# Seven weight slots, each at an address offset of its own, in a float32 transformer kernel on one core

## The chip, the cores and the metric

The kernel runs on one NeuronCore of a Trainium2 chip. The metric is the device time of one execution in microseconds, from the first instruction to the last with what lies around them. The engines are TensorE (PE in the profile; its weight loads are the row PEld), VectorE (DVE), ScalarE (ACT), GpSimd (POOL) and SyncE (SP), which here only issues loads. SBUF is the on-chip memory of 128 partitions in which all operands of this case lie.

## What is computed

Three transformer blocks follow each other on 256 tokens of width 2048, all in float32. The first is attention (two kinds of heads, with 256 tokens of context beside), the second a Fourier mixer, the third a mixer of a gated delta rule and dilated attention, with a convolutional gated MLP behind it. Cut to the lines that hold nearly all of the arithmetic, the reference is a row of products of activations with weight matrices:

```python
def attn_project(h, ...):            # first block, for x and for ctx
    z = h @ w_in                     # 2048 x 4928
def gated_out(y_a, y_b, gate, w_out):
    return (y * jax.nn.silu(gate)) @ w_out
def fourier_mixer(h, w_in, w_out):   # second block
    u, gate = jnp.split(h @ w_in, 2, axis=-1)          # 2048 x 8192
    f = jnp.fft.fft2(ug, axes=(1, 3), norm="ortho").real
    return (f * jax.nn.silu(gate)) @ w_out             # 4096 x 2048
def token_mixer(n, ...):             # third block
    proj = jnp.einsum("bsd,dp->bsp", n, w_in)          # 2048 x 13344
    ...
    return jnp.einsum("bsm,md->bsd", mixed, w_out)
def conv_gated_mlp(n, w_ffn_in, conv_ffn_w, w_ffn_out):
    up = depthwise_conv_centered(jnp.einsum("bsd,df->bsf", n, w_ffn_in), conv_ffn_w)  # 2048 x 11264
    gate, val = jnp.split(up, 2, axis=-1)
    return jnp.einsum("bsf,fd->bsd", jax.nn.silu(gate) * val, w_ffn_out)              # 5632 x 2048
```

## The kernel before, in words

**Units.** All weights of these products are packed on the host into 478 units of at most 1 MB: 128 partitions by up to 2048 float32, which is four slices of 128 input rows by 512 output columns, or two or three slices of 768 columns. `UNITS` (line 206) is the list in the order in which they are used, and each of the engines' programs walks through it in this order.

**Slots.** SBUF is one slab of 53,100 float32 per partition. Its first 7 × 2048 words are the weight slots, laid out by `W.place(UNIT)` (lines 466 to 468): four raw ones, into which units are loaded, and three high ones. Behind them are a region `K` of 9360 words that is kept through the kernel, and a region `R` that each block lays out anew; activations are there, each buffer at a multiple of 8 words from the region's start (`place`, line 449). Unit number u uses raw slot u modulo 4 and high slot u modulo 3 (`RAW_OF`, `HIGH_OF`, lines 264 and 265). In the head (the first 44 units) there are six raw slots and four high ones: two more raw slots and one more high slot lie in `R`, the high one at word 40080 of the slab, the raw ones at words 42128 and 51048 (lines 504 to 511); there the slots go by u modulo 6 and u modulo 4.

**A unit's way.** SyncE waits until the raw slot's previous unit is used and loads the next one (line 621). ScalarE casts it to float32r, a shortened float32, into the high slot (`act_hi`, line 1155). VectorE subtracts the high part from the raw one and writes the rest, also float32r, over the raw slot (`dve_lo`, line 1665). Both run two or three units ahead of TensorE. The activations are split in the same way into a high and a low half, for most of the kernel in `Hhi` and `Hlo` (words 27792 and 23696 of the slab). TensorE (`pe_unit`, lines 648 to 652) then does three matmuls for each slice and each 128 output columns:

```python
hi = unit_cut(high[HIGH_OF[u]][1], u)[:, kt - k0, :]
lo = unit_cut(raw[RAW_OF[u]][1], u)[:, kt - k0, :]
mm(e, o, *operands(kt, i, hi, 0), first, False)
mm(e, o, *operands(kt, i, hi, 1), False, False)
ins = mm(e, o, *operands(kt, i, lo, 0), False, last)
```

For most products the 128 × 128 piece of weights is the stationary operand (loaded by a LDWEIGHTS of its own) and the activations are the moving one, of 256 columns. For the products `fu`, `dv` and a few others it is the other way round. Each matmul instruction of the trace has one weight load in front of it, which TensorE does while the matmul before it runs.

**Order.** Nothing is planned at run time: each engine's program is written out, with semaphores between. Smaller work (norms, attention, the Fourier products, the delta rule) stands between units of the long products or in gaps of its own. The last stretch, `ff` and `oX` from 2601 us on, is 6,336 matmuls of 256 columns with nothing between them.

Of the kernel before, what the change touches and what calls it, by code (L numbers as in the profile page):

```python
# [9 lines left out]
F32 = mybir.dt.float32  # L10
F32R = mybir.dt.float32r
# [8 lines left out]
UNIT = 2048  # L20
SLOTS = 4
HIGH = 3
A_SCALE = (128 + 64) ** -0.5
B_SCALE = 128 ** -0.5
SLAB = 53100
KEEP = 9360
ALPHA = 4.0 ** 0.25
EPS = 1e-6
# [367 lines left out]
def program(nc, a, out, cmaps):  # L396
    with ExitStack() as ctx:
# [7 lines left out]
        base = -(-nc.sbuf_base // 32) * 32  # L405
        ctx.enter_context(nc.sbuf_tensor("slab", [128, SLAB], F32))
        pieces = {}

        def piece(o, n, dt):
            if (o, n, dt) not in pieces:  # L410
                name = f"{'r' if dt == F32R else 'f'}_{o}_{n}"
                pieces[(o, n, dt)] = nc.alloc_sbuf_tensor_at(name, [128, n], dt, offset=base + 4 * o)
            return pieces[(o, n, dt)]
# [49 lines left out]
                named["all"] = v  # L463
                return named

        W = Region(0, UNIT * (SLOTS + HIGH))
        raw = [W.place(UNIT) for _ in range(SLOTS)]
        high = [W.place(UNIT) for _ in range(HIGH)]
        K = Region(W.size, KEEP)
        R = Region(W.size + KEEP, SLAB - KEEP - W.size)  # L470

# [1893 lines left out]
```

## Time and profile before

| | us |
|---|---|
| median of the timed runs (three) | 3376.86 |
| lowest and highest of them | 3375.43, 3382.23 |
| profiled execution, its own time | 3346.91 |
| its span, first to last instruction | 3345.1 |
| TensorE busy in it | 3122.8 |
| VectorE busy | 1871.0 |
| ScalarE busy | 1266.4 |

The profiled execution is one more execution of the same program; what lies around its span is 1.8 us. Busy time is the union of an engine's instructions. Matmuls overlap in the trace, since the next one begins before the one before has drained: a stretch in which TensorE is busy throughout can still be denser or less dense. How dense it is, is told by the count of matmuls in a window of known width. A count in a window includes the instructions that reach over its edges, two or three more than begin in it.

### The profile page before, as it was taken

The numbers are of one execution on the slowest core, as the hardware profiler recorded it, in microseconds if no ns is written. First come the engines' busy times: TensorE is split into PE (matmuls) and PEld (weight loads), VectorE is DVE, ScalarE is ACT, GpSimd is POOL, SyncE is SP. The second block draws the span as 40 slices with busy tenths as digits, with TensorE's granted clock in tenths as the row PEclk, the third lists the DMA queues.
The fourth block names the chain that finished last, engine by engine and source line by source line (L and its number), as shares of the span: only waits on it lengthen the run. The fifth ranks groups of instructions, "written<-read, shape, count | busy, mean of one in ns | idle before, by whom it ended". The sixth has DMA issues, their size and how long they took to land.

```text
span 3345.1 us, 52152 instructions
## 1 busy us (share of the span) xinstructions
PE 3122.8 (93%) x23130; PEld 2854.4 (85%) x23130; DVE 1871.0 (56%) x2119; ACT 1266.4 (38%) x1310; POOL 211.2 (6%) x180
## 2 busy tenths in 40 slices
PE   6999879987899999979999999999979899999998
PEld 3699765586888998969999989978869899999998
DVE  6736664465765434455545444764544666557753
ACT  7623231133333333343433333432223444334433
POOL 0000000000000000001112110013400000000000
PEclk9999899998999999999999998999989999999999
DMA  8745544343465454424444434520004455555553
GB/s 333 290 168 216 189 167 155 126 175 149 189 247 193 173 183 161 150 100 161 162 155 151 159 125 152 186 92 1 1 28 174 156 197 187 195 199 191 199 188 130
DMA packets 81632, 548.01 MB, mean 164 GB/s; under 512 B 9568, under 2 KB 9600, under 8 KB 28160
## 3 DMA queue, kind: packets, MB, share of 16 engines
q1 hardware_dynamic: 69984, 466.91, 39.3%
q0 software_dynamic: 9216, 67.11, 5.4%
q10 hardware_dynamic: 2208, 10.65, 0.8%
q8 instruction: 183, 3.00, 0.4%
q14 instruction: 41, 0.34, 0.0%
HBM read 542.54 MB, written 2.10 MB: 163 GB/s over the span
## 4 chain that ended last, share of the span: by engine, by line
PE 86%; DVE 6%; issue 3%; DMA 3%; ACT 2%; SPq 0%; DVEq 0%; ACTq 0%
PE bank L631 84%; DMA f<-in_later 2%; DVE f L1694 1%; DVE r L1665 1%; ACT r L1155 1%; PE bank L679 1%; DMA f<-in_units 1%; PE bank L920 0%; DVE f L1882 0%; DVE f L1713 0%; DVE f L2091 0%; ACT f L1267 0%; DVE f L1980 0%; DVE f L1904 0%; DVE f L1836 0%
## 5 line engine op out<-in xcount | busy, mean ns | idle before, releaser
L631 PE MATMUL bank<-r,r 128*128 128x256 f32 (+4 forms) x19360 | 2427.8, 287 | 88.0 <-issue 41.5
L631 PEld LDWEIGHTS bank<-r,r 128*128 128x128 f32 (+3 forms) x19360 | 2320.9, 188 | 192.4 <-issue 103.8
L1665 DVE TENSOR_TENSOR r<-f,r 128x2048 fp32r<-128x2048 f32 (+2 forms) x466 | 1012.6, 2175 | 915.8 <-ACT r L1155 914.4
L1155 ACT CAST r<-f 128x2048 fp32r<-128x2048 f32 (+2 forms) x466 | 835.7, 1795 | 1057.5 <-PE bank L631 856.4
L631 PE MATMUL bank<-f,f 128*128 128x128 f32 (+10 forms) x3258 | 660.5, 356 | 82.7 <-ACT f L1334 14.8
L631 PEld LDWEIGHTS bank<-f,f 128*128 128x128 f32 (+5 forms) x3258 | 474.2, 195 | 211.4 <-issue 112.3
L1694 DVE SCALAR_TENSOR_TENSOR f<-f,f,f 128x512 f32<-128x512 f32 x240 | 180.2, 751 | 52.1 <-DMA f<-in_later 45.3
L1167 ACT COPY f<-bank 128x512 f32<-128x512 f32 (+2 forms) x141 | 80.3, 588 | 152.4 <-PE bank L631 146.7
L2029 DVE SCALAR_TENSOR_TENSOR f<-f,f,f 128x255 f32<-128x255 f32 (+1 forms) x272 | 131.6, 484 | 9.7
L679 PEld LDWEIGHTS bank<-f,f 128*128 128x128 f32 x288 | 39.3, 166 | 69.1 <-issue 24.2
L2280 POOL DMA_DIRECT2D f<-in_later x64 | 34.0, 531 | 1013.9 <-DVE f L1694 844.4
L679 PE MATMUL bank<-f,f 128*128 128x128 f32 x288 | 51.5, 321 | 39.8 <-ACT f L1316 13.8
L2289 POOL TENSOR_TENSOR f<-f,f 32x512 f32<-32x512 f32 x24 | 30.9, 1286 | 821.2 <-PE bank L631 821.2
L1316 ACT ACTIVATE f<-bank,f 128x512 f32<-128x512 f32 x32 | 22.0, 688 | 153.1 <-DVE f L1843 146.6
L2307 POOL TENSOR_TENSOR f<-f,f 128x512 f32<-128x512 f32 x56 | 72.3, 1315 | 54.6 <-PE bank L631 48.8
L2097 DVE TENSOR_TENSOR f<-f,bank 128x512 f32<-128x512 f32 x48 | 33.0, 688 | 71.7 <-PE bank L631 71.7
L2292 POOL TENSOR_TENSOR f<-f,f 32x512 f32<-32x512 f32 x24 | 63.0, 2626 | 1.9
L1456 ACT COPY f<-bank 128x512 f32<-128x512 f32 x48 | 28.1, 586 | 89.4 <-PE bank L631 89.4
L1334 ACT ACTIVATE f<-f 128x512 f32<-128x512 f32 x48 | 29.8, 629 | 79.6 <-DVE f L1877 48.7
L1836 DVE TENSOR_REDUCE f<-bank 128x1 f32<-128x512 f32 x32 | 22.0, 689 | 65.2 <-PE bank L631 65.1
L1385 ACT ACTIVATE f<-f,f 128x768 f32<-128x768 f32 x16 | 15.0, 938 | 80.8 <-DVE f L1988 80.8
L1267 ACT ACTIVATE f<-f 128x256 f32<-128x256 f32 (+1 forms) x46 | 19.1, 433 | 58.9 <-PE bank L631 29.6
(160 smaller groups left out, 879.9 us busy)
## 6 DMA issues: line engine op xcount, KB each, us to landing
f<-in_units SPq DMA_DIRECT2D x346, 1024.0 KB, 4.8
f<-in_units SPq DMA_DIRECT2D x120, 768.0 KB, 4.3
f<-in_later POOLq DMA_DIRECT2D x64, 1024.0 KB, 5.5
f<-in_units SPq DMA_DIRECT2D x8, 576.0 KB, 5.0
f<-in_x ACTq DMA_DIRECT2D x2, 1024.0 KB, 13.0
f<-in_ctx ACTq DMA_DIRECT2D x2, 1024.0 KB, 11.4
f<-in_x_turned ACTq DMA_DIRECT2D x1, 2048.0 KB, 11.4
out<-f SPq DMA_DIRECT2D x8, 256.0 KB, 2.4
```

The lines of the kernel that those rows point to most:

```text
L631: return e.matmul(o, lhsT, rhs, start=start, stop=stop, skip_group_check=True)
L679: ins = e.transpose(o[:, j * 128:(j + 1) * 128], src(j), ident)
L1155: e.copy(unit_view(high[HIGH_OF[u]][1], u), unit_view(raw[RAW_OF[u]][0], u)).then_inc(*up("w_hi", ("hi", u)))
L1167: return e.copy(dst, src(ps("lin", name, q))).then_inc(*up("act_out", ("out", "lin", name, q), *names))
L1665: e.tensor_tensor(unit_view(raw[RAW_OF[u]][1], u), unit_view(raw[RAW_OF[u]][0], u), unit_view(high[HIGH_OF[u]][1], u).bitcast(F32), ALU.su ...
L1694: ins = e.scalar_tensor_tensor(o, own[:, kt, :], s, o, ALU.mult, ALU.add)
L2029: ins = e.scalar_tensor_tensor(o[:, lo:hi], s[:, lo + d:hi + d], tap(j), o[:, lo:hi], ALU.mult, ALU.add)
L2097: e.tensor_tensor(gXT[:, n, :], gXT[:, n, :], ps("dXT", dr, l, n)[:, :], ALU.subtract).then_inc(*up("dve_delta", ("out", "dXT", dr, l, n), ...
L2280: e.dma_start(own, a["later"][n // 4, n % 4].rearrange("p (k c) -> p k c", k=4)).then_inc(*up("own_slot", ("own landed", n), by=16))
L2289: e.tensor_tensor(v, v, cos2.unsqueeze(1).to_broadcast([32, 2, T]), ALU.mult).then_inc(*up("pool_dil"))
L2292: e.tensor_tensor(v, v, two(rt[n % 2][0:32, :]), ALU.add).then_inc(*up("pool_dil", ("roped half", x, hf, br), ("half", n)))
L2307: e.tensor_tensor(v4(gL[:, m, :]), v4(gAT[:, m, :]), b4(ec[f"{lev}{l}"]), ALU.mult).then_inc(*up("pool_delta", ("L", dr, l, m)))
```

## The change

The slots no longer lie at multiples of 2048 words. Slot i lies at i × 2048 words plus a shift of its own, out of a list of seven. The tensors that the program declares start at multiples of 8 words, so where a shift is not one, the tensor starts 4 words earlier and the slot is a slice of it. The region of the slots becomes 64 words longer, the slab too, and the regions `K` and `R` begin 64 words (256 bytes) later. The sizes of the slots, the instructions and their order, the semaphores and the queues stay as they are; so do the three further slots of the head, apart from the 64 words.

```diff
-SLAB = 53100
+SLAB = 53164
+SHIFTS = (8, 24, 36, 40, 44, 56, 64)
@@
-        W = Region(0, UNIT * (SLOTS + HIGH))
-        raw = [W.place(UNIT) for _ in range(SLOTS)]
-        high = [W.place(UNIT) for _ in range(HIGH)]
+        W = Region(0, UNIT * (SLOTS + HIGH) + 64)
+        slots = []
+        for i, s in enumerate(SHIFTS):
+            o, skip = i * UNIT + s // 8 * 8, s % 8
+            slots.append(tuple(piece(o, UNIT + skip, dt)[:, skip:skip + UNIT] for dt in (F32, F32R)))
+        raw, high = slots[:SLOTS], slots[SLOTS:]
```

## Rows read from the trace of the kernel before

**Rows 1.** The page: span, and busy time by engine with its share of it.

```profile
span 3345.1 us, 52152 instructions
...
PE 3122.8 (93%) x23130; PEld 2854.4 (85%) x23130; DVE 1871.0 (56%) x2119; ACT 1266.4 (38%) x1310; POOL 211.2 (6%) x180
```

**Rows 2.** The chain that ended last: its engines; pieces (start us, us, what).

```profile
PE 86%; DVE 6%; issue 3%; DMA 3%; ACT 2%; SPq 0%; DVEq 0%; ACTq 0%
...
3.48 22.49 DMA f<-in_units
...
856.41 228.47 PE bank L631 x1520
...
1388.80 79.49 PE bank L631 x656
...
2601.06 725.25 PE bank L631 x6360
```

**Rows 3.** Groups by form, whole span (count, then busy us, mean ns, idle before).

```profile
L631 PE MATMUL bank<-r,r 128*128 128x256 f32 x18144 | 2148.1, 280 | 64.9 <-issue 41.5 <-DVE r L1665 11.1 <-ACT f L1167 7.4
...
L631 PE MATMUL bank<-r,r 128*128 128x512 f32 x768 | 184.7, 398 | 0.0
```

**Rows 4.** Two windows, all engines: us, busy (x count), clock, DMA share, GB/s.

```profile
2050.00:2200.00 150.00, 150.00 (x1276) 150.00 (x1275) 114.06 (x153) 70.49 (x73) 0.00 (x0) 1.00 0.53 185
2860.00:3190.00 330.00, 330.00 (x2914) 330.00 (x2913) 204.66 (x206) 137.64 (x101) 0.00 (x0) 1.00 0.56 194
```

**Rows 5.** Groups by form in the window 2050 to 2200 us.

```profile
L631 PE MATMUL bank<-r,r 128*128 128x256 f32 x1276 | 150.4, 279 | 0.0
...
L1665 DVE TENSOR_TENSOR r<-f,r 128x2048 fp32r<-128x2048 f32 x27 | 61.9, 2292 | 30.3 <-ACT r L1155 30.3
L1155 ACT CAST r<-f 128x2048 fp32r<-128x2048 f32 x27 | 51.6, 1910 | 59.3 <-PE bank L631 47.8 <-DMA f<-in_units 11.5
```

**Rows 6.** Groups by form in the last stretch, 2601 to 3326 us.

```profile
L631 PE MATMUL bank<-r,r 128*128 128x256 f32 x6336 | 719.8, 276 | 13.2 <-issue 13.2
...
L1665 DVE TENSOR_TENSOR r<-f,r 128x2048 fp32r<-128x2048 f32 x117 | 268.2, 2292 | 232.8 <-ACT r L1155 231.7
L1155 ACT CAST r<-f 128x2048 fp32r<-128x2048 f32 x117 | 224.0, 1914 | 313.6 <-PE bank L631 294.6 <-DMA f<-in_units 19.0
```

**Rows 7.** Timeline of TensorE, 1545 to 1565 us (start us, us, what, count).

```profile
1548.01 4.35 PE L631 MATMUL bank<-r,r 128*128 128x256 f32 x36
1552.29 1.04 PE L631 MATMUL bank<-f,f 32*32 32x512 f32 x2
1553.26 4.51 PE L631 MATMUL bank<-r,r 128*128 128x256 f32 x36
```

**Rows 8.** Timeline of ScalarE, casts of units 5 and 6 in the head.

```profile
26.00 1.90 ACT L1155 CAST r<-f 128x2048 fp32r<-128x2048 f32 x1 [0.60 <-DMA f<-in_units]
28.48 1.91 ACT L1155 CAST r<-f 128x2048 fp32r<-128x2048 f32 x1 [0.58 <-DMA f<-in_units]
```

**Rows 9.** Timeline of VectorE, the subtraction of the same unit 5.

```profile
27.93 2.29 DVE L1665 TENSOR_TENSOR r<-f,r 128x2048 fp32r<-128x2048 f32 x1 [0.21 <-ACT r L1155]
```

**Rows 10.** DMA issues: count, KB each, median us to landing.

```profile
f<-in_units SPq DMA_DIRECT2D x346, 1024.0 KB, 4.8
```

**Rows 11.** Timeline of TensorE in the head: units 17, 28, 29, 40, 41, 43.

```profile
82.93 4.05 PE L631 MATMUL bank<-r,r 128*128 128x256 f32 x33
...
119.03 4.04 PE L631 MATMUL bank<-r,r 128*128 128x256 f32 x33
...
125.60 4.09 PE L631 MATMUL bank<-r,r 128*128 128x256 f32 x34
...
159.73 5.34 PE L631 MATMUL bank<-r,r 128*128 128x256 f32 x44
...
165.15 4.17 PE L631 MATMUL bank<-r,r 128*128 128x256 f32 x34
...
173.75 5.46 PE L631 MATMUL bank<-r,r 128*128 128x256 f32 x45
```

## Prediction

> **What bounds the kernel.** I read the page first: TensorE is busy for 93% of the span, VectorE for 56%, ScalarE for 38% [rows 1]. The chain of waits then says that TensorE's own work is 86% of what set the end; its long pieces are unbroken matmul streams, the last of them 725 us long [rows 2]. The groups by form say what they consist of: 18,144 float32r matmuls of 256 columns, each with a weight load of its own out of a slot [rows 3]. So the time hangs on the spacing of these matmuls, and I worked that out from windows that hold nothing else: width over count, less the two or three instructions that a window's edges count twice.
>
> It is not one spacing but two. From 2050 to 2200 us, 150/(1276−2.4) = 117.8 ns; from 2860 to 3190 us, 330/(2914−2.4) = 113.3 ns, and both are kept without a break [rows 4]. The clock is at 1.00, that is 2.4 GHz, in both, and the operation and tiles are the same. The other engines don't make the difference: ScalarE's cast takes 1.91 us in both stretches, VectorE's subtraction 2.29 [rows 5, 6], and the DMA engines' share is 0.53 in the slow one and 0.56 in the fast one [rows 4]. The clearest place is around 1550 us: two neighbouring units of `dk`, 36 matmuls each, the same buffers for activations, the same start behind two small matmuls. One takes 4.35 us, the next 4.51 [rows 7]: 0.16/36 = 4.4 ns per matmul, the whole distance between the levels. 
>
> About 7,800 of the 18,144 are at the low level: the 6,336 of the last stretch [rows 6], some 600 of the 656 from 1388.8 us on, some 480 at the start of the piece from 856.4 us [rows 2], and a few short units like the one in [rows 7]. The rest, some 10,300, are at the high one.
>
> **The basis of the sum.** The profiled execution took 3346.9 us (span 3345.1), the timed ones 3376.9 in the median, 30 us more. If the last stretch had fallen onto the high level in the timed runs, that would be 6,336 × 4.4 ns = 28 us. That fits but isn't shown. I take it: the base is then 3376.9 with nearly all of the 18,144 at 117.8 ns.
>
> **The change, part by part.** No instruction, semaphore or queue entry is added, removed or moved. Only addresses change.
>
> 1. The places. From the slab's start, all seven slots were at multiples of 8192 bytes. They now lie 32, 96, 144, 160 bytes (the four raw ones) and 176, 224, 256 bytes (the three high ones) past them. Modulo 128 these are 32, 96, 16, 32, 48, 96, 0: five different places, not seven; seven different ones they are modulo 256. Everything behind the slots moves by 256 bytes and keeps its place modulo 128 and 256. The activation buffers (word 27792 and others of the same sort) lie 64 bytes past a multiple of 128. So the distance from weights to activations changes, differs between the two weights of a triple (high, high, raw), and changes at each unit.
>
> 2. ScalarE's cast, VectorE's subtraction. The head has a natural test: its sixth raw slot is at word 51048, 32 bytes past a multiple of 128. Its first unit, the sixth of the kernel, is cast at 26.00 us in 1.90 us, the next one, out of a slot at a multiple, in 1.91 us [rows 8], and it is subtracted at 27.93 us in 2.29 us [rows 9], the mean of the other stretches [rows 5, 6]. Nothing for places of 32 bytes; for 16 no row exists. If they cost 5%, 0.1 us per unit, the cover is a subtraction and cast of 4.2 us in a unit of 5.4 us in which ScalarE then waits for TensorE (294.6 us of waiting in the last stretch) [rows 6]: nothing reaches the end.
>
> 3. The loads. 1 MB lands in 4.8 us [rows 10], and of the cast's waits in the last stretch 19.0 us are for a load [rows 6], with two more units already split ahead of TensorE. A row of 8192 bytes that starts off its place could cost a 32nd more, 0.15 us: covered. Only the first 30 us, where the chain waits 22.5 us for loads [rows 2], have no cover: 1 us at most. A gain is excluded there, as nothing lies better than before.
>
> 4. TensorE's reads. This is the whole sum. The head again has the nearest rows, units whose two weights lie at different places (raw slot at 64 or 32 bytes past, or high slot at 64). Their spacings, (length−0.28)/(count−1) with 0.28 us for the last one's own length [rows 5, 6]: 117.8, 117.5, 115.5, 117.7, 117.9, 117.7 ns [rows 11]. The first, third and fifth are out of the 32-byte slot: 117.8, 115.5, 117.9. None is at 113.3, none above 117.9. So a mixed place makes neither a new high nor the low level, but there is a level between. After the change every unit is of this mixed kind, in twelve combinations. I give the level between one third and the high one two thirds: (115.5 + 2×117.6)/3 = 116.9 ns. Against 117.8: 0.85 ns × 18,144 = 15 us less. The 768 matmuls of 512 columns read weights as the moving operand in their pairs [rows 3]; at the same share (0.7%) of 0.18 ms that is 1 us. 3376.9 − 15 − 1 = 3361 us. The bounds: if all fell onto the level between, 2.3 ns × 18,144 = 42 us less (3335); the two slots at 16 bytes past a multiple of 32 (raw 2, high 0) are in no row. They serve 1/12 + 2/9 = 31% of the matmuls; I bound them by zero and by once more the distance of the levels, 4.4 ns × 5,540 = 24 us more (3401 if nothing is gained).
>
> **A rule that speaks against it.** The rows show two spacings for the same matmul with all the rest alike [rows 4, 7]. The Trainium skill ("SBUF — State Buffer", Who interferes with whom) says that TensorE has two independent read ports, one for the moving operand and one for weight loads, and that it never waits on anyone. By that rule the change is worth exactly nothing, 3376.9 us. The trace doesn't bear out the rule for this pair of reads, since the high level exists, but it doesn't show either that places decide the level: it is the second rival.
>
> **Rivals.**
> - All-low. Places that differ keep the two reads apart in every unit: 18,144 at 113.3 ns, 4.45 × 18,144 = 81 us less, 3296 us. For it: the level exists and holds for 725 us [rows 2]. Against it: none of the six mixed units reaches it [rows 11].
> - Nothing. The level is drawn at the start of a stream by its phase, as in [rows 7] at unchanged places: 3370 to 3383 us, with 3376.9 as its time. For it: five of six mixed units at the usual high level [rows 11].
> - Slower, the low level lost. Place: the last stretch, 6,336 matmuls. If the timed runs have it at the low level, as the profiled one does (the 30 us are then something else), the mixed places throw it to about 117: 3.7 × 6,336 = 23 us more, and with nothing gained elsewhere, 3400 us. It decides from the point where the low level of the last stretch is in the base. The 16-byte slots of point 4 end at the same time. For it: the low level is the profile's own state there [rows 6]; against it, the 30 us.
> - That the change doesn't do what it says: it doesn't modulo 128, as worked out above, but the distances do change, so this has no time of its own.
>
> Taken instead against the profile's own time, the forecast's level gives +3.6 × 7,800 = 28 and −0.85 × 10,300 = −9: 3346.9 + 19 = 3366 for an execution like the profiled one. So a profile of the changed kernel may well be longer than that of before although the timed runs are shorter.
>
> **How the numbers follow.** Forecast (level between in a part of the units) 0.35, own range 3340 to 3370; nothing 0.29; slower 0.27; all-low 0.09. The measurement of this kernel can tell about 0.2%, 6.8 us, so faster is below 3370.1 and slower above 3383.6: faster 0.35 + 0.09 = 0.44, same 0.29, slower 0.27. The range leaves out all-low and the far part of slower: 3332 to 3402.
>
> **What would show it.** In windows of the last stretch (now 113.3) and of 2050 to 2200 us (now 117.8), the spacing of the 256-column matmuls: forecast, both between 115.5 and 117.8 and changing from unit to unit; all-low, 113.3 in both; nothing, whole stretches at one of the old levels, though perhaps at others than before. Cast 1.91 and subtraction 2.29 us unchanged would show point 2 right; landing at 4.8 us point 3. A spacing above 118 in units of raw 2 or high 0 would show the 16-byte cost. The prediction is wrong at its root if the timed 30 us are not TensorE's level in the last stretch, or if the level proves free of places.

## The result, and the profile after

| | before | after |
|---|---|---|
| timed, us | 3377.61 median (3375.43 to 3382.23) | 3401.32 median (3397.57 to 3403.76) |
| profiled execution, us | 3346.9 | 3403.7 |

The ratio is 1.0067, 95% interval 1.005 to 1.0085: the change makes the kernel 24 us slower. The forecast was 3361.0, faster, so the sign was wrong. The stated range (3332 to 3402) holds the median by 0.7 us only, and that end came from the bound for the 16-byte slots and from a rival, not from the forecast.

The page of after, span and busy time, answers to [rows 1]:

```profile
span 3401.9 us, 52152 instructions
...
PE 3184.7 (94%) x23130; PEld 2913.9 (86%) x23130; DVE 1871.9 (55%) x2119; ACT 1262.6 (37%) x1310; POOL 211.4 (6%) x180
```

Counts are unchanged, VectorE and ScalarE too. TensorE alone has grown. Pieces of the chain of after (start, us, what), which answer to [rows 2]:

```profile
863.40 231.62 PE bank L635 x1520
...
2620.00 763.28 PE bank L635 x6360
```

The last stretch took 725.25 us before and takes 763.28 now, 38.0 us more. The other piece took 228.47. Windows of after with the columns of [rows 4], then the groups by form with those of [rows 3] (whole span) and of [rows 6] (2620 to 3384 us):

```profile
2050.00:2200.00 150.00, 150.00 (x1253) 150.00 (x1253) 108.72 (x142) 66.67 (x67) 0.00 (x0) 0.99 0.52 183
2860.00:3190.00 330.00, 330.00 (x2769) 330.00 (x2768) 192.57 (x193) 128.12 (x95) 0.00 (x0) 1.00 0.53 184
```

```profile
L635 PE MATMUL bank<-r,r 128*128 128x256 f32 x18144 | 2211.2, 284 | 65.2 <-issue 41.5 <-DVE r L1669 10.5 <-ACT f L1171 7.3
L635 PE MATMUL bank<-r,r 128*128 128x512 f32 x768 | 183.9, 397 | 0.0
```

```profile
L1669 DVE TENSOR_TENSOR r<-f,r 128x2048 fp32r<-128x2048 f32 x117 | 268.2, 2293 | 266.9 <-ACT r L1159 266.8
L1159 ACT CAST r<-f 128x2048 fp32r<-128x2048 f32 x117 | 223.0, 1906 | 344.9 <-PE bank L635 326.2 <-DMA f<-in_units 18.7
```

Worked out as before the change: 150/(1253−2.4) = 119.9 ns where 117.8 was, and 330/(2769−2.4) = 119.3 ns where 113.3 was (the first at a granted clock of 0.99). The spacing is no longer one number within a stretch. It changes from unit to unit. Timeline of TensorE in after, clipped to single units of the last stretch: the unit with raw slot 144 and high slot 224, the next but one (32 and 176), and a later one (144 and 256):

```profile
2645.07 6.37 PE L635 MATMUL bank<-r,r 128*128 128x256 f32 x50
...
2656.69 6.05 PE L635 MATMUL bank<-r,r 128*128 128x256 f32 x50
...
2668.12 6.06 PE L635 MATMUL bank<-r,r 128*128 128x256 f32 x50
```

With (length−0.28)/(count−1) these are 124.3, 117.8 and 118.0 ns; each row takes in one or two matmuls of the neighbours. From the starts of the single matmuls inside each unit, over 135 of the 136 units of the last stretch, the spacing is the same within 0.2 ns each time a pair of slots comes back:

| ns per matmul | raw 32 | raw 96 | raw 144 | raw 160 |
|---|---|---|---|---|
| high 176 | 117.8 | 118.7 | 120.0 | 118.9 |
| high 224 | 120.0 | 120.8 | 124.45 | 119.3 |
| high 256 | 117.8 | 117.8 | 117.8 | 117.8 |

(Places in bytes past a multiple of 2048 words; the activations lie 64 bytes past a multiple of 256, and 256 is the old place modulo 256.) The mean is 119.3, against 117.8 for the high level of before: 1.5 × 18,144 = 27 us, and 24 were measured. So the table carries the loss, if the timed runs of before sit at the high level. That, and what the table's numbers belong to, is what the runs were for.

### The profile page after: what moved, and what is told of

Its sections match the earlier page's. It is cut to its first block, busy times and chain, and to the rows that moved or that the text cites. A ratio compares the mean times of both kernels' runs of the same rounds, so it can differ in the third digit from the quotient of the medians.

```text
span 3401.9 us, 52152 instructions
## 1 busy us (share of the span) xinstructions
PE 3184.7 (94%) x23130; PEld 2913.9 (86%) x23130; DVE 1871.9 (55%) x2119; ACT 1262.6 (37%) x1310; POOL 211.4 (6%) x180
## 4 chain that ended last, share of the span: by engine, by line
PE 86%; DVE 6%; issue 3%; DMA 3%; ACT 2%; SPq 0%; ACTq 0%; DVEq 0%
PE bank L635 84%; DMA f<-in_later 2%; DVE f L1698 1%; DVE r L1669 1%; ACT r L1159 1%; DMA f<-in_units 1%; PE bank L683 1%; PE bank L924 0%; DVE f L1886 0%; DVE f L1717 0%; DVE f L2095 0%; ACT f L1271 0%; DVE f L1984 0%; DVE f L1908 0%; DVE f L1840 0%
## 5 line engine op out<-in xcount | busy, mean ns | idle before, releaser
L635 PE MATMUL bank<-r,r 128*128 128x256 f32 (+4 forms) x19360 | 2493.6, 291 | 85.9 <-issue 41.5
L635 PEld LDWEIGHTS bank<-r,r 128*128 128x128 f32 (+3 forms) x19360 | 2384.1, 189 | 192.5 <-issue 107.5
L635 PEld LDWEIGHTS bank<-f,f 128*128 128x128 f32 (+5 forms) x3258 | 471.6, 194 | 212.3 <-issue 113.3
L1971 DVE TENSOR_TENSOR f<-bank,f 32x512 f32<-32x512 f32 x24 | 16.3, 679 | 47.3 <-PE bank L635 47.3
```

The source lines that it names most:

```text
L635: return e.matmul(o, lhsT, rhs, start=start, stop=stop, skip_group_check=True)
```

## The experiments

Two theories stood at first: that the last stretch of before is at the high level when it is timed (the basis of the sum), and that the new spacings come from the distance between the two weights of a triple, or from the high slot's place alone. For each run I read the chain's last piece. All hold the same 6,336 matmuls of 256 columns, and the piece of 725.25 us was at 113.33, so a piece gives its mean spacing as 113.33 + (piece − 725.25)/6.336 ns; this agrees with the starts of the single matmuls to 0.2 ns.

**The kernel before, unchanged, and three partial changes.** `same` has no edit.

> The kernel before, unchanged. In its first profile the last stretch (6,336 matmuls of 256 columns) took 725 us, 113.3 ns each, and the execution 30 us less than the timed ones. Theory A (a stream at equal places falls onto 113.3 or 117.8 ns by its start, and the timed runs have the last stretch at 117.8): 3375 to 3382 us timed; the profile has the last stretch at 725 or at 747 us, and its own time is 3347 or about 3375 accordingly. Theory B (the 30 us lie elsewhere, such as around the span): the last stretch stays at 725 us in an execution whose own time is about 3377.

3374.83 us, ratio 0.9999 [0.9986, 1.0011]. The last piece, and the two windows of [rows 4], in its profiled execution:

```profile
2592.71 753.41 PE bank L631 x6360
```

```profile
2050.00:2200.00 150.00, 150.00 (x1326) 150.00 (x1325) 117.09 (x154) 72.14 (x74) 0.00 (x0) 1.00 0.55 194
2860.00:3190.00 330.00, 330.00 (x2805) 330.00 (x2804) 195.05 (x194) 131.76 (x98) 0.00 (x0) 1.00 0.53 187
```

The same program has the two levels the other way round: 150/(1326−2.4) = 113.3 ns in the window that had 117.8, and 117.8 in the one that had 113.3. The last piece is 28.2 us longer than in [rows 2]. So the program doesn't fix the level; it differs from execution to execution. The profiled execution behind the prediction had the low level in the longest stretch, which is rare by the times: 31 timed runs of before ran from 3341.53 to 3384.17 us with the median at 3375.37, and of these and the ten of `same` two were below 3350 us, all others at 3366.64 or above. This execution took 3366.64 us with some 2,200 matmuls at the low level by their starts. At the high level they would add 2,200 × 4.45 ns = 10 us: 3376 us, the median of the timed runs. The basis of the sum held as far as two profiles and these times can tell; in the other timed runs the stretch itself wasn't seen.

`raw_only` moves the four raw slots alone:

```diff
-SHIFTS = (8, 24, 36, 40, 44, 56, 64)
+SHIFTS = (8, 24, 36, 40, 64, 64, 64)
```

> Only the four raw slots are shifted, by 32, 96, 144 and 160 bytes; the three high slots are all 256 bytes on, which is their old place modulo 256. Theory A (the spacing is set by the pair of places of a unit's two weights, and the high one, read twice in three, decides): as in the units of the changed kernel whose high slot was at 256, 117.8 ns with every raw slot; the last stretch 6,336 x 117.8 = 746 us, never 725; timed 3377 us, like before. Theory B (each misplaced slot costs by its own share): the raw slots serve one third of the matmuls, so a third of the change's 24 us, 3385 us and 118.3 ns.

3376.95 us, ratio 1.001 [1.0001, 1.0019]. `high_only` moves the three high ones alone:

```diff
+SHIFTS = (0, 0, 0, 0, 44, 56, 64)
```

> Only the three high slots are shifted, by 176, 224 and 256 bytes; the raw ones are at their old places. Theory A (the high place decides): nearly the whole loss of the change, last stretch about 119.2 ns, 755 to 763 us, timed 3395 to 3401 us. Theory B (each slot by its own share): two thirds of it, 3393 us. Theory C (only the 16-byte places cost): high 0 alone pays, a third of the units, timed 3385 us.

3377.69 us, 1.0022 [0.9996, 1.0048]. `all_256` moves all seven by 256 bytes:

```diff
+SHIFTS = (64, 64, 64, 64, 64, 64, 64)
```

> All seven slots 256 bytes on, so that nothing changes modulo 256, neither place nor distance; slab, kept region and the rest as in the change. Theory A (places modulo 128 or 256 count): like the kernel before in both of its states, 3377 us within 0.3% timed, last stretch 725 or 747 us in the profile. Theory B (that everything lies 256 bytes further on costs by itself): part of the 24 us stays, 3385 us or more.

3375.14 us, 0.9992 [0.9972, 1.0011]. The last pieces of the three, in this order:

```profile
2605.90 753.12 PE bank L635 x6360
```

```profile
2599.31 753.33 PE bank L635 x6360
```

```profile
2602.64 753.41 PE bank L635 x6360
```

All are at 117.8 ns, and the starts say so for every raw slot in the first and every high slot in the second. Neither half of the change costs anything that counts. So none of the three numbers expected for `high_only` came, and the theory that the high place decides, which had the number of `raw_only` right, falls with it. So the high slot's place alone isn't it, and the distance between the two weights isn't either, for these two runs hold distances of 0 to 224 bytes. In these runs the cost needs both weights off the old place. That fits the bottom row of the table, in which one of them is at it. It isn't enough, though: raw 32 with high 176 is off in both and has 117.8.

**All seven slots alike, at other places.** `all_16`, `all_32`, `all_64` and `all_96` take the distance between the weights away and change only the one to the activations. The first is shown; the others have 8, 16 and 24 words:

```diff
-SHIFTS = (8, 24, 36, 40, 44, 56, 64)
+SHIFTS = (4, 4, 4, 4, 4, 4, 4)
```

> All seven slots 16 bytes on: the two weights of a unit at equal places, but both moved against the activations. So far either of the two weights could be moved alone without loss (last stretch 753 us, 117.8 ns, in both), and both together lost 6 x 6,336 / 1000 = 10 us beyond that. Theory A (a unit loses when both its weights lie off the old distance to the activations): spacing above 117.8, 118 to 124 ns, last stretch 755 to 790 us. Theory B (it loses when its two weights lie apart from each other and neither is at the old place): 117.8 or 113.3 ns, 753 or 725 us.

> All seven slots 32 bytes on. Theory A (distance to the activations): above 117.8 ns, last stretch over 755 us. Theory B (distance between the two weights): 117.8 or 113.3 ns, 753 or 725 us.

> All seven slots 64 bytes on, to the same place modulo 128 and 256 as the activations. Theory A: this takes the old distance of 64 bytes away altogether, so the largest effect of the four, up or down; over 755 us or steadily 725. Theory B: 753 or 725 us like before.

> All seven slots 96 bytes on, 32 bytes past the activations' place. Theory A: above 117.8 ns, over 755 us, and if only the size of the distance counts, the same as with 32 bytes. Theory B: 753 or 725 us.

Single executions of 3370.32, 3370.71, 3411.55 and 3390.29 us; the kernel before, also run once beside them, took 3388.51, so only the spacings can be compared here, not the times. Last pieces, one kernel a fence:

```profile
2602.91 746.84 PE bank L635 x6360
```

```profile
2603.09 747.05 PE bank L635 x6360
```

```profile
2623.76 767.37 PE bank L635 x6360
```

```profile
2611.54 758.20 PE bank L635 x6360
```

By the starts: 116.7, 116.7, 120.00 and 118.3 ns. For 16 and 32 bytes neither expected range came: they lie between the two levels of before. (The 10 us in the expectation of `all_16` are 763.3 − 753.3; the product beside them is a slip.) The place of slots that all lie alike moves the spacing by itself, and it is worst of these four where weights and activations lie at the same place modulo 256 (64 and 64).

`act_64` asks whether that is the distance or the place as such. The slots go back and everything behind them is moved:

```diff
-SHIFTS = (8, 24, 36, 40, 44, 56, 64)
+SHIFTS = (0, 0, 0, 0, 0, 0, 0)
-        W = Region(0, UNIT * (SLOTS + HIGH) + 64)
+        W = Region(0, UNIT * (SLOTS + HIGH) + 48)
```

> All seven slots are back at multiples of 2048 words, and everything behind them (the activations too) lies 64 bytes earlier than in the changed kernel and 192 bytes later than in the kernel before. If the distance between weights and activations sets the spacing, this is the distance of the run with all slots at 64 bytes: 120.00 ns in every unit, a last piece of about 767 us. If the place of the weights in the memory alone sets it, the last piece is the one of the kernel before, 725 or 753 us (113.3 or 117.8 ns).

3413.25 us in its one execution, 120.00 ns in every unit:

```profile
2624.56 768.14 PE bank L635 x6360
```

With the slots at their old places the kernel is as slow as `all_64`. At this distance at least, it is the distance that decides, not the weights' place. `all_112` and `all_192` (28 and 48 words) fill in two more:

```diff
-SHIFTS = (8, 24, 36, 40, 44, 56, 64)
+SHIFTS = (28, 28, 28, 28, 28, 28, 28)
```

> All seven slots lie 112 bytes beyond a multiple of 2048 words. Between the runs at 96 bytes (118.39 ns) and at 256 (117.78): if the distance alone sets the spacing with all slots alike, it is between 113 and 120 ns, and the last piece 725 to 767 us; a spacing of 124 would say that a distance that isn't a multiple of 32 bytes costs by itself.

> All seven slots 192 bytes beyond a multiple of 2048 words, which puts them 128 bytes from the activations modulo 256. Uniform places so far gave 113.33 or 117.78 (64 bytes from the activations), 116.65 or 120.0 (48), 116.67 (32), 120.00 (0), 118.39 (32 on the other side) and 123.33 ns (48 on the other side). If the distance alone decides, this run gives one constant between 113 and 124 ns, a last piece of 725 to 790 us; it is asked whether any place is always at 113.3, which would make a kernel some 50 us faster than before.

3429.1 and 3400.8 us in one execution each, 123.33 and 118.67 ns in the last stretch:

```profile
2618.95 789.61 PE bank L635 x6360
```

```profile
2620.13 760.27 PE bank L635 x6360
```

No place was always at 113.3. 112 bytes is outside the range expected for it. It is a multiple of 16 and not of 32 and costs the most, but 16 itself is among the cheapest, so the odd 16 bytes are no cost by themselves. Nor is 123.33 the one spacing of this place. Two windows of `all_112`, one before the last stretch and one at its very end:

```profile
2060.00:2190.00 130.00, 130.00 (x1106) 130.00 (x1106) 100.88 (x137) 61.99 (x64) 0.00 (x0) 1.00 0.53 187
3392.00:3402.00 10.00, 10.00 (x84) 10.00 (x83) 0.00 (x0) 0.00 (x0) 0.00 (x0) 1.00 0.00 0
```

130/(1106−2.4) = 117.8 ns, so 112 bytes has two levels as well. The second window settles a rival. Moved slots also move what ScalarE and VectorE write and where loads land, and the delay could have been theirs. For these 10 us no other engine works and the DMA share is 0.00, and the starts still have 123.33 ns in every unit: the delay, once there, is within TensorE's own stream. That the other engines have a part in which level a stretch falls onto is not excluded.

`all_16_timed` is `all_16` again, timed, as one of the two places that looked better than before.

> All seven slots 16 bytes beyond a multiple of 2048 words, now timed. One execution had 116.64 ns in the last stretch, between the two levels of the kernel before. If the timed runs of the kernel before sit at 117.8 in that stretch (and in most of the others), this one is faster by about (117.8 - 116.6) x 6,336 = 7 us there and up to 20 us over all 18,144 matmuls: 3356 to 3370 us. If the kernel before is often at 113.3, there is no difference.

3375.99 us, 1.0004 [0.9979, 1.0029], single runs from 3365.74 to 3396.99: no gain, where 3356 to 3370 us had been expected. The window 2060 to 2190 us says why, first in `all_16`, then in `all_16_timed`:

```profile
2060.00:2190.00 130.00, 130.00 (x1116) 130.00 (x1116) 107.25 (x144) 59.62 (x61) 0.00 (x0) 1.00 0.54 187
```

```profile
2060.00:2190.00 130.00, 130.00 (x1086) 130.00 (x1085) 100.73 (x138) 59.86 (x63) 0.00 (x0) 1.00 0.53 184
```

130/(1116−2.4) = 116.7 ns against 130/(1086−2.4) = 120.0, in the same kernel. This place has two levels too, 116.7 and 120.0, and a stretch falls onto either. (`all_32` ran its last stretch at 116.7 and had 117.7 from 2510 to 2580 us.)

**The costliest pair.** `pair_worst` gives every unit the raw place 144 and the high place 224:

```diff
+SHIFTS = (36, 36, 36, 36, 56, 56, 56)
```

> All four raw slots lie 144 bytes and all three high slots 224 bytes beyond a multiple of 2048 words, the pair of places that in the changed kernel ran at 124.45 ns per 256-column matmul. If the spacing belongs to the pair of places, every matmul of the last stretch takes 124.45 ns, its chain piece of 6,360 matmuls is about 796 us, and the kernel is at about 3376 + (124.45 - 117.78) x 18,144 = 3497 us. If the cost belonged to the mixing of places from unit to unit, which is absent here, the spacing is 117.8 and the time about 3376 us.

3421.48 us, 1.0134 [1.0116, 1.0152], and the last piece:

```profile
2629.06 768.15 PE bank L635 x6360
```

120.00 ns, neither of the two numbers expected. So a pair's places don't fix the spacing. The same execution shows it within itself, for in one stretch of `gate` the pair did run as in the changed kernel, (10.98−0.28)/86 = 124.4 ns:

```profile
401.79 10.98 PE L635 MATMUL bank<-r,r 128*128 128x256 f32 x87
```

In the changed kernel the same pair in a unit that starts behind other work (`gate`) has 6.02 us for 48 matmuls with one gap of 0.22 us among them, (6.02−0.28−0.22)/46 = 120.0 ns:

```profile
330.31 6.02 PE L635 MATMUL bank<-r,r 128*128 128x256 f32 x48
```

So this pair has two levels, 120.0 and 124.45. The theory then was that the unit ahead chooses. Three runs test it. `reversed` keeps all twelve pairs and changes what precedes each:

```diff
-        raw, high = slots[:SLOTS], slots[SLOTS:]
+        raw, high = slots[:SLOTS][::-1], slots[SLOTS:]
```

> The changed kernel with its raw slots taken in the reverse order: the same seven places, the same twelve pairs of a raw and a high slot, but each pair now follows another one. Theory that the pair alone sets the spacing: the unit with the raw slot at 144 and the high slot at 224 bytes keeps 124.45 ns, the others keep 117.8 to 120.7, and the last piece of 6,360 matmuls is again about 763 us; time about 3401 us. Theory that the unit ahead matters too (two levels to each pair, chosen at entry): that pair falls to 120.00 or others rise by 4.4 ns, and the last piece moves by some us to either side.

3401.02 us, 1.0077 [1.006, 1.0094]. Its last piece, and one unit of the costly pair:

```profile
2620.89 760.74 PE bank L635 x6360
```

```profile
2731.70 6.15 PE L635 MATMUL bank<-r,r 128*128 128x256 f32 x50
```

(6.15−0.28)/49 = 119.8: the pair fell to 120.00, in 11 units of 11. Of the other eleven means one moved clearly, that of high 224 with raw 96, from 120.8 to 120.0; the rest stayed within 0.5 ns. The time is that of the change: losing the one costly pair is worth 4.4/12 = 0.4 ns or 2.3 us in the last stretch (763.28 to 760.74), which timing can't tell. `raws_144` and `highs_224` keep the pair and one rotation each; their lists, in this order:

```diff
-SHIFTS = (8, 24, 36, 40, 44, 56, 64)
+SHIFTS = (36, 36, 36, 36, 44, 56, 64)
```

```diff
-SHIFTS = (8, 24, 36, 40, 44, 56, 64)
+SHIFTS = (8, 24, 36, 40, 56, 56, 56)
```

> All raw slots at 144 bytes, the three high slots as in the change (176, 224, 256 bytes). In the changed kernel these three pairs ran at 120.00, 124.45 and 117.78 ns. If a pair alone sets its spacing, these return: mean 120.74 ns, last piece about 772 us. If rotation of the raw slot is what lifted the middle one, it is 120.00: mean 119.3, last piece about 763 us.

> All high slots at 224 bytes, the raw slots as in the change (32, 96, 144, 160 bytes). In the changed kernel these four pairs ran at 120.00, 120.68, 124.45 and 119.41 ns: mean 121.1, last piece about 775 us, if a pair alone sets its spacing. If rotation of the high slot is what lifted the third, it is 120.00, mean 120.0, last piece about 768 us.

3401.62 and 3425.82 us, one execution each. The last piece and a unit of the pair, `raws_144` first:

```profile
2617.68 763.53 PE bank L635 x6360
```

```profile
2642.98 6.04 PE L635 MATMUL bank<-r,r 128*128 128x256 f32 x49
```

```profile
2630.83 774.43 PE bank L635 x6360
```

```profile
2655.96 6.01 PE L635 MATMUL bank<-r,r 128*128 128x256 f32 x47
```

(6.04−0.28)/48 = 120.0 with the raw slots all alike, (6.01−0.28)/46 = 124.6 with the raw slot changing from unit to unit in the change's order (124.0 in the mean; 30 of its 34 units are at 124.45, four at 119.9). The pair has two levels 4.4 ns apart, like the old place. The four exceptions tell what chooses. The unit ahead of this pair always has raw 96 and high 224 here. It is at 120.5 to 120.7 ns ahead of each of the 30, and at 117.8 ahead of three of the four (the fourth opens the stretch). First the unit ahead of the row just shown, then a unit ahead at the other level and its follower:

```profile
2650.02 5.84 PE L635 MATMUL bank<-r,r 128*128 128x256 f32 x47
```

```profile
2946.83 5.70 PE L635 MATMUL bank<-r,r 128*128 128x256 f32 x47
2952.61 4.35 PE L635 MATMUL bank<-r,r 128*128 128x256 f32 x35
```

(5.84−0.28)/46 = 120.9 is followed by 124.6, (5.70−0.28)/46 = 117.8 by (4.35−0.28)/34 = 119.7. The slots are the same in both cases, so it is the level of the unit ahead that is handed on, not its places alone. The other two pairs of `highs_224` (120.2 and 119.2 ns) are within 0.2 ns of the changed kernel's, and so are the other two of `raws_144`.

## Why the prediction was wrong, by its own steps

- **What bounds the kernel.** Right. Nothing but the spacing moved, and the kernel moved with it.
- **The basis.** Right by all that the runs show: timed, the last stretch is as a rule at 117.8 ns (`same`), so 3376.9 already contains it. Whoever had compared the two profiled executions (3346.9 and 3403.7) would have found a loss of 57 us, of which more than half is the draw of one execution.
- **Points 1 to 3** (places, cast and subtraction, loads). Right: the cast takes 1.91 us, the subtraction 2.29, and 1 MB lands in 4.8 us in the median, also with slots 16 bytes past a multiple of 32. DMA issues of after, answering to [rows 10]:

```profile
f<-in_units SPq DMA_DIRECT2D x346, 1024.0 KB, 4.8
```

- **Point 4, TensorE's reads.** This step failed. It took 116.9 ns for every mixed unit from six units of the head [rows 11] and closed with "none above 117.9". The six rows were read rightly, but they were of another kind: in each, one of the two weights lay at the old place and only the other was off it. `raw_only` and `high_only` are that kind throughout, and they behave as the rows did: no gain, no loss. In the changed kernel eight of the twelve pairs have both weights off, and for these no row of before existed. The sentence "After the change every unit is of this mixed kind" is where two kinds became one. The level between that I gave to a third of the units was a single unit at 115.5 ns (unit 29), and it was a second level of its slots and not their spacing: in `same` the units 17 and 41, out of the same 32-byte slot, have 115.6 ns and unit 29 has 117.9. Units 17 and 29 of `same`, (4.21−0.28)/34 and (4.29−0.28)/34:

```profile
81.30 4.21 PE L631 MATMUL bank<-r,r 128*128 128x256 f32 x35
124.01 4.29 PE L631 MATMUL bank<-r,r 128*128 128x256 f32 x35
```

The mean over the last stretch came out at 119.3, not 116.9: (119.3−116.9) × 18,144 = 44 us, against the 40 us between forecast and result. The step also named the head's slots by their places modulo 128 (its "32-byte slot" is 160 bytes past a multiple of 256), and that doesn't name a place: all slots at 64 bytes gave 120.00 ns, all at 192, which is 64 modulo 128, gave 118.67.
- **The 1 us for the 768 wide matmuls.** 184.7 to 183.9 us of busy time: right, and without weight.
- **The bounds.** The 24 us more for the slots at 16 bytes past a multiple of 32 gave the right end for a reason that is only half right. Raw 144 with the old high place costs nothing (117.8), and high 224 with raw 96, both multiples of 32, costs 3.0 ns.
- **The rivals.** "Slower, the low level lost" gave 3400 us and the time is 3401, but by its mechanism it is refuted: it needed the last stretch at the low level in the timed runs of before, and `same` has it at the high one. What was right in it is that mixed places can be worse than the old one; its price of 23 us in one stretch stood for 1.5 ns in all of them. "Nothing" holds for half the change and not for the whole. "All-low" never appeared.
- **The rule.** In the prediction it stood against any effect of places. The rows first: kernels that differ in nothing but the common place of the slots ran their last stretch at 116.7 to 123.33 ns, and moving only the activations gave 120.00. The Trainium skill ("SBUF — State Buffer", Who interferes with whom) has the moving operand's and the weight load's ports independent. By it all would be equal; the runs don't bear it out for float32r matmuls whose weights are loaded anew for each.

Shown: the loss is TensorE's spacing; with the activations where they are it needs both weights away from the old place; the common place of all slots moves the spacing; a pair of places can have two levels, and the level of the unit ahead can choose between them; no other engine's work is needed to keep a slow spacing up (the window at the end of `all_112`). Not shown: why a place has the levels it has. There is no rule that gives the table's twelve numbers, and that the distance between weights and activations alone counts was tried at one distance (none, `act_64` against `all_64`, one execution each). That the two reads hold each other up inside the SBUF is argued, not seen.

## What to carry to other kernels

Before a spacing measured on some units is given to others, list what is the same in them: here the rows at hand had one of the two weights moved, the change moved both. When one execution and the median of the timed ones differ by more than the timed ones differ among themselves, look for a stretch whose pace differs between executions of the same program, and measure the unchanged kernel again before crediting a change. And when a TensorE stream loads weights for every matmul, the addresses of weights and activations modulo 256 bytes can be worth some 5% of a stretch (117.78 to 123.33 ns here): keep a distance that was measured to be good, and give it to all slots.

## What the runs showed of the hardware that was not expected

- Float32r matmuls of 256 columns, each with its own weight load, out of slots that all lay alike, kept a spacing within 0.2 ns over hundreds of microseconds at a granted clock of 1.00, and that spacing was one of a few: 113.33, 116.7, 117.78, 118.3, 118.7, 120.00, 123.33 ns.
- At five settings of the places the same program ran at either of two levels: 113.33 or 117.78 (the old one), 116.7 or 120.0 (16 bytes), 116.7 or 117.7 (32 bytes), 117.8 or 123.33 (112 bytes), 120.0 or 124.45 (raw 144, high 224).
- A unit can hand its level on: with the same slots in both units, raw 144 with high 224 ran at 124.45 ns behind a unit at 120.7 and at 119.9 behind one at 117.8 (`highs_224`).
- A slow spacing holds without any other engine: 123.33 ns stayed while ScalarE, VectorE, GpSimd and the DMA engines all stood at 0.00 (`all_112`, 3392 to 3402 us).
- Weights at the activations' place modulo 256 bytes: always 120.00 in the last stretch. 48 bytes beyond it: 123.33, the slowest of the uniform places; 48 bytes ahead of it, 116.7 in the last stretch of both executions.
- Moving one of the two weights of a triple left 117.78 in the last stretch in all six pairs that were seen; moving both gave 117.8 to 124.45.
